# HGRN level scores in column tiles: six of seven levels as two 128x64 halves per head pair

## The reference: what is computed

```python
def step(s, xs):                       # one chunk
    qc, kc, lfc, vc = xs
    cum = jnp.cumsum(lfc, axis=-2)
    o_inter = jnp.einsum('bhtk,bhkv->bhtv', qc * jnp.exp(cum), s)
    diff = cum[:, :, :, None, :] - cum[:, :, None, :, :]
    decay = jnp.where(causal, jnp.exp(jnp.minimum(diff, 0.0)), 0.0)
    scores = jnp.einsum('bhtsk,bhsk->bhts', qc[:, :, :, None, :] * decay, kc)
    o = o_inter + jnp.einsum('bhts,bhsv->bhtv', scores, vc)
```

## Time and profile before

| | |
|---|---|
| median of 3 runs | 967.33 us (966.66 to 967.97) |
| the profiled execution | 967.89 us |
| its span in the profile | 966.1 us |
| PE busy | 938.3 us (97% of the span) |
| DVE, ACT, POOL busy | 531.1, 394.6, 238.7 us |
| section B's four iterations | about 123 to 275 us of the span |
| granted TensorE clock over the span | 0.993 |

### The profile page before, as it was taken

How to read it: one execution, slowest core, us unless ns; L and a number is a source line. 1 busy time by engine, 2 the same in 40 slices (tenths; PEclk the granted TensorE clock), 3 DMA queues, 4 the chain that set the end, 5 groups by cost and what they waited for, 6 DMA issues and landing times.

```text
span 966.1 us, 20940 instructions
## 1 busy us (share of the span) xinstructions
PE 938.3 (97%) x7834; PEld 916.1 (95%) x7834; DVE 531.1 (55%) x632; ACT 394.6 (41%) x524; POOL 238.7 (25%) x280
## 2 busy tenths in 40 slices
PE   6999999999999999999999999999999999999995
PEld 6999998998999999899999999999999999999994
DVE  5322267677656545566566555666566343435453
ACT  5432355455445445423334444444443222222433
POOL 0007066756411011000551111111111031212331
PEclk9999999999999999999999999999999999999997
DMA  7133522212233233354232322223323433322202
GB/s 238 50 101 91 175 71 72 76 54 66 65 99 93 85 105 109 102 177 121 88 88 72 103 88 87 87 87 97 98 87 95 121 90 90 90 87 82 82 29 94
DMA packets 168053, 91.49 MB, mean 95 GB/s; under 512 B 13585, under 2 KB 166561, under 8 KB 167601
## 3 DMA queue, kind: packets, MB, share of 16 engines
q1 hardware_dynamic: 149698, 80.61, 28.1%
q10 hardware_dynamic: 18320, 10.42, 3.8%
HBM read 83.10 MB, written 8.00 MB: 94 GB/s over the span
## 4 chain that ended last, share of the span: by engine, by line
PE 94%; ACT 2%; DVE 1%; issue 1%; DMA 1%; ACTq 0%; SPq 0%; DVEq 0%
PE acc L476 82%; PE lvb L554 3%; DMA xtok<-in_x_prompt 1%; PE lvb L666 1%; PE mb L678 1%; ACT zq L889 1%; PE lvb L517 1%; PE ob L603 0%; PE mb L590 0%; ACT L941 0%; PE ob L656 0%; PE mb L660 0%; PE ob L598 0%; PE lvb L637 0%; PE ob L655 0%
## 5 line engine op out<-in xcount | busy, mean ns | idle before, releaser
L1118 DVE TENSOR_TENSOR wlo<-raw,whi 128x1024 fp32r<-128x1024 f32 (+2 forms) x132 | 193.0, 1463 | 179.0 <-ACT whi L798 179.0
L798 ACT ACTIVATE whi<-raw 128x1024 fp32r<-128x1024 f32 (+2 forms) x132 | 146.5, 1111 | 352.5 <-PE acc L476 351.4
L476 PE MATMUL acc<-xah,whi 128*128 128x260 f32 x896 | 186.9, 290 | 0.0
L476 PE MATMUL acc<-xah,wlo 128*128 128x260 f32 x896 | 180.3, 283 | 0.0
L476 PE MATMUL acc<-xal,whi 128*128 128x260 f32 x896 | 179.9, 282 | 0.0
L476 PE MATMUL acc<-xbh,whi 128*128 128x260 f32 x832 | 168.6, 284 | 3.2 <-DVE tg L1475 2.4
L476 PE MATMUL acc<-xbh,wlo 128*128 128x260 f32 x832 | 167.7, 283 | 0.0
L476 PE MATMUL acc<-xbl,whi 128*128 128x260 f32 x832 | 167.4, 283 | 0.0
L476 PEld LDWEIGHTS acc<-xah,whi 128*128 128x128 f32 x896 | 137.9, 189 | 9.0 <-issue 8.2
L476 PEld LDWEIGHTS acc<-xah,wlo 128*128 128x128 f32 x896 | 137.9, 188 | 0.0
L476 PEld LDWEIGHTS acc<-xal,whi 128*128 128x128 f32 x896 | 137.8, 188 | 0.0
(11 more groups left out here) (285 smaller groups left out, 1230.2 us busy)
## 6 DMA issues: line engine op xcount, KB each, us to landing
raw<-in_w_in SPq DMA_DIRECT2D x96, 256.0 KB, 3.1
raw<-in_w_up SPq DMA_DIRECT2D x88, 256.0 KB, 3.1
raw<-in_w_down SPq DMA_DIRECT2D x16, 384.0 KB, 3.2
raw<-in_w_down SPq DMA_DIRECT2D x16, 320.0 KB, 3.7
raw<-in_w_out SPq DMA_DIRECT2D x16, 256.0 KB, 3.0
raw<-in_w_ple_gate SPq DMA_DIRECT2D x8, 512.0 KB, 3.7
x_transposed<-xstg SPq DMA_DIRECT2D x1, 2080.0 KB, 7.6
hT<-x_transposed ACTq DMA_DIRECT2D x1, 2080.0 KB, 9.8
```

What stands on the lines that cost most here:

```text
L476: mm = pe.matmul(acc[tile % 2][:, b, 0:HT], wt[slot][:, w], xx[:, c, b * HT:(b + 1) * HT], start=first and i == 0 and q == 0, stop=last an ...
L798: act.activation(whi[k % 2][:, 0:n], raw[k % 2][:, 0:n], ACT.Copy).then_inc(hi_ready, 1)
L1118: dve.tensor_tensor(wlo[k % 2][:, 0:n], raw[k % 2][:, 0:n], whi[k % 2][:, 0:n].bitcast(fp), SUB).then_inc(lo_ready, 1)
```

## The change

For levels 0 to 5 each matmul of a head pair becomes two: keys 0 to 63 by the 32 queries of that half for both heads, and keys 64 to 127 by the other 32 queries for both heads. Each has 64 weight columns and 64 moving columns (two runs of 32), and writes its own half of the partitions. Level 6 keeps one matmul of a head pair, with keys 0 to 63 only (at this level the keys are all in the first half) and all 128 moving columns. The score blocks that no longer get computed are those which the merge's masks leave out. Nothing else changes: waits, semaphores, the merge, ACT's and POOL's work stay as they are.

```diff
                 for l in levels:
                     for c in range(4):
-                        mm = pe.matmul(lvb[:, l % 2, c * 128:(c + 1) * 128], lk[l % 4][:, c, :],
-                                       zq[l % 4][:, c].rearrange("k two t -> k (two t)"), start=True, stop=True)
+                        out = lvb[:, l % 2, c * 128:(c + 1) * 128].rearrange("s (two t) -> s two t", two=2)
+                        if l == LV - 1:
+                            mm = pe.matmul(out[0:64], lk[l % 4][:, c, 0:64], zq[l % 4][:, c], start=True, stop=True)
+                            continue
+                        for r in range(2):
+
+                            mm = pe.matmul(out[64 * r:64 * r + 64, :, 32 * r:32 * r + 32],
+                                           lk[l % 4][:, c, 64 * r:64 * r + 64],
+                                           zq[l % 4][:, c, :, 32 * r:32 * r + 32], start=True, stop=True)
                     mm.then_inc(sc_full, 1)
```

## The result

The changed kernel takes 974.86 us (median of 4 runs, 974.38 to 975.14) against 967.00 us of the kernel before beside it (966.49 to 967.97). The ratio is 1.0078, with a 95% interval from 1.0062 to 1.0094: slower by 0.8%, 7.9 us, where 4.4 us less were forecast. The profiled execution has a span of 972.8 us against 966.1.

The account below looks back on a forecast made before the run. PE was taken to bound the kernel (94% of the span). The first iteration saves 1.13 us, the other three 1.08 each (3.24), together 4.4 off 967.33: 962.9 us, range 961.3 to 965.4.

Parts of the forecast that it names:

- prices of PE: Scores on PE: 32 records at 0.029 us, a use of two levels 1.08 us after idle, 1.19 behind running matmuls.
- use 2's wait of about 0.6 in the first iteration: Before use 2, PE waits 0.57 us for ACT's packing of levels 4 and 5.
- the end of the merge in the first iteration: Merge of levels 0 and 1 before use 1 ends 0.40 us earlier, at 128.79, so PE does not wait.
- Use 3: Last scores use of an iteration: level 6 in one column tile loses 0.25 us through entry, exposed load and exit.
- Two runs of 32 columns: Moving columns read and written in two runs in the scores: taken to keep L607's pace, 0.029 us per record.
- the first of the two waits: Merge of levels 0 and 1 before use 1: in iterations 2 to 4 use 0's 0.70 us buys no earlier use 1.
- 0.7 us of idle time per iteration: Before use 1 in iterations 2 to 4, PE stands idle 0.7 us more, waiting for DVE's merge.
- ACT's chain: Rival before use 2: packing levels 4 and 5 stays at 172.94, gain 2.0 us in all, 965.3 us; chance 0.12.
- pace: Rivals on scores' record pace: gain eaten around 0.046 us, 967.3 us, chance 0.04; slower at 0.058, 971.8 us, chance 0.05.
- overlap: Rival in the scores: column tiles don't overlap at all, 0.087 us per record, 983 us; chance 0.01.
- The rule weighed in the prediction: Trainium skill, for PE's scores: weight loads overlap matmuls only in different row groups; the prediction followed L607's trace instead.
- uses 1 and 2: Scores on PE in iterations 2 to 4: use 1 saves 0.78 us, use 2 saves 0.55 us.

Follow-up runs that it names:

- the run with level 6 whole: Changed kernel with POOL's sample products moved from before level 4 to behind level 7, and level 6 in whole tiles again: 961.28 us, ratio 0.9940.
- the pause given back: Changed kernel with one more wait on POOL, for its own sample products (vblk), in front of level 4: 963.86 us against 967.07, ratio 0.9965.
- the move: POOL's sample products put behind level 7 instead of before level 4: on the changed kernel 961.82 us, on the kernel before 967.02, both against 967.84.

## Why the prediction was wrong

Its prices of PE hold. The records of L554 became 384 of L560 and 32 of L556, 416 together; a use takes 1.08 to 1.09 us where 1.08 was put; use 2's wait of about 0.6 in the first iteration (0.41), 1.13 us saved there (1.19), the end of the merge in the first iteration in time. Use 3 lost 0.17 by the traces (2.31 us from the diagonal to the next unit against 2.14), or 0.21 by the run with level 6 whole, where 0.25 was put. Two runs of 32 columns cost nothing. With the pause given back the sum comes out: 4.8 us of section B against 4.4. By the whole time it is 3.2 us less (963.9; 1.8 to 4.9 by its interval), where 962.9 was forecast.

**The step that failed** is in the first of the two waits under "What ends later in its place": DVE's work ahead of the merge "hangs on the end of unit 3 of the iteration before, which keeps its distance to use 0". The prediction carried over the duration of the copy as if it were DVE's own. It was 1.87 us for 8 columns, which alone says that it is a wait; the 0.17 of the like operations behind it show the work. It ended with POOL's vblk, and could end there because POOL then paused for PE's scores, which are what the change makes faster. The row with the pause was in the trace, with PE's line as its releaser, and POOL was read only for whether it was late. The description of the chip at the start of this document has the same gap: it says that the engines meet only through semaphores, and here DVE's copy stood behind POOL's instructions without one. The rivals looked for lateness as well: ACT's chain, pace, overlap. None was that an engine released earlier gets in the way of a third.

**The second, smaller failure** is that idle time was priced at its length. The prediction had 0.7 us of idle time per iteration and left the clock out; at 2.3 us it fell in three of three iterations here, and cost 1.5 us each time on top (4.40 against 2.87). So in the second iteration a saving of 1.1 turned into a loss of 2.2: use 1 comes 1.81 us later behind use 0 and the clock costs 1.53, 3.34 together; uses 1 and 2 save 0.78 and 0.55 and use 3 loses 0.17, 1.16 net. That leaves 2.18, and 2.23 was measured. With the copy short the idle time was 0.42 and the clock stayed, so this term mattered only because the first step failed.

**The rule weighed in the prediction** ended as the rows had it: column tiles in the same rows do load and multiply at the same time, at 0.029 us a record. The rule that mattered was another one of the Trainium skill, "SBUF — State Buffer", section Who interferes with whom: DVE (in a form that uses two ports) and GpSimd share one pair of ports, and whichever is first holds it for its whole instruction while the other blocks. The traces agree in that the copy ends just behind the end of a POOL instruction each time, 0.02 to 0.10 us behind it. That POOL's instructions hold the copy back is shown by the runs; that a pair of ports is the reason is what the page says, and no run here shows the ports. The page does not say who is next when both want it; here DVE got in at some boundaries and missed four in a row at others.

## What to carry to other kernels

Before an engine is released earlier, ask what its next instructions will overlap, and read small operations with long durations as waits: 8 columns in 1.87 us are a wait for another engine, and its end may hang on a pause that the change takes away. A gain on the busiest engine is worth what the next waits leave; when it turns into idle time, look at the granted clock behind it too. Where two engines block each other, look for a place for the long instruction of the one that has time to spare: here the move cost nothing in the kernel before (967.02 us against 967.84) and secured the gain in the changed one.

## What was not expected of the hardware

A DVE operation of 8 columns took 3.8 us beside POOL, in 12 of 12 iterations of four kernels in which POOL's `vblk` of 2.1 to 2.2 us was followed by level 4 without a pause, and 1.0 in 6 of 6 where the POOL instruction in front was half as large. PE's granted clock fell to 0.50 behind idle times of 2.3 us before use 1 in 8 of 9 iterations of three kernels, behind 2.03 us in the one such iteration, behind 1.85 to 1.87 in one of three, and never in section B behind 1.4 or less. Filling an idle stretch of PE with matmuls whose results are thrown away made a kernel 4.9 us faster.
